# A two-layer trunk with three token mixers on eight cores: the Silu inputs of the branches computed as seven block products

## The chip, the cores and the metric

The program runs on the eight NeuronCores of one Trainium2 chip. Each core computes 1024 of the 8192 tokens, with 62 tokens of left context (a halo), and the cores don't talk to each other. The metric is the device time in microseconds (us) of the slowest core. TensorE (PE) multiplies matrices into PSUM (8 banks of 128 x 512 float32), VectorE (DVE) and ScalarE (ACT) do the elementwise work, the queue of GpSimd (POOL) issues the loads of the weights, SyncE (SP) the other transfers. Each engine runs its own instructions in the order in which the program emits them.

## The reference

```
for each of 2 layers:
  xn = RMSNorm(h)                                # h: tokens x 2048
  proj = xn @ W_in                               # 9 slices of 1024 columns, 3 gates of 2048
  A: y_A = silu(z_A) * B * conv3(C * x_in)
  B: y_B = silu(z_B) * scale * group_linear(trailing_mean_w(u) - u),  w in (2,4,8,16)
  C: y_C = silu(LayerNorm(dwconv31(value * sigmoid(gate)))) * silu(z_C)
  merged = sum over the branches of sigmoid(g_b) * (y_b @ W_branch_out_b)
  h = h + merged @ W_o
  h = h + sigmoid(h @ W_ple_gate) * (p_i @ W_ple_proj)
final RMSNorm
```

The change is about the three inputs z_A, z_B and z_C of silu: products of xn (2048 deep) with 1024 columns of W_in each.

## The kernel before, in words

Channels lie on partitions and tokens along the free axis. xn is 16 tiles of 128 channels x TL = 1086 tokens in bf16. Layer 0 needs 1056 output columns of each tile (LO = 30), layer 1 needs 1024 (LO = 62).

**Plain projection** (`mm_group`, line 308): a tile of 128 output channels is 16 matmuls deep (k = 0..15), over 3 pieces of 352 columns in 3 PSUM banks (layer 0) or 2 of 512 in 2 banks (layer 1). `next_pg` hands out banks in turn. One load (`load_main`, three ring slots) brings the weights of two tiles, which are written "a pair" or "j" here.

**Seven block products** (`block_group`, line 594): a pair is a 2 x 2 block product (two output tiles, two halves of the depth, two halves of the tokens), and one level of Strassen-Winograd makes it from seven products instead of eight: 7 x 8 x 2 matmuls of 264 columns in layer 0 (`nb` = 2), 7 x 8 of 512 in layer 1. It needs sums of the weights, made on VectorE by `weight_sums` (four operations, one of them in place in the ring slot) into the shared `sb`, and sums of xn, made once for each layer by `xsum` into `tb`. On TensorE its products go in the order b0, b4, b1, b0, b2, b1, b2 (banks). In between, ScalarE copies p1 <- p0 ahead of the third product, then saves p4, copies p2 <- p1 ahead of the fifth, applies the function to g00 and saves `u3`. VectorE makes g01 and g11 (two TT) after the sixth product, and ScalarE applies the function to g10; the function on g01 and g11 waits in `pend`. Before the change only the 24 pairs of merge gates of a layer were done in this way (`merge_branch`, line 659), all with Sigmoid.

**Merge of a branch**: for q = 0..3 two gate pairs as block products, then four groups (jj) of 8-deep matmuls of yb, whose PSUM VectorE multiplies by the gate into `acc` (branch A) or into a scratch tile and then adds (B, C). Weight sums of the next gate pair come after the first block, and at jj = 1; those of a branch's first pair stand at the head of `merge_branch`.

**Background taps**: the 31-tap convolution of branch C runs on VectorE. `conv_tap` operations (8 tiles x 31) stand in a queue `bgq`, and `bg(n)` emits the next n at that place of VectorE's order. Eight `xsum` operations are put at the queue's head when branch A begins. `bg(len(bgq))` (line 826) emits all that are left before branch C's LayerNorm, which needs the last tap of the last tile: V(7).

**Branch A** (line 729): for j = 0..3 projections x and C (pieces of 353 or 342), then B, then z: two plain groups, `ACT Silu` from PSUM into Tt, and a product into yb on VectorE. bg(3), bg(1), bg(3), bg(3) follow the tiles of the four projections.

**Branch B** (line 769): u (two tiles, 3 banks each), pooling on VectorE, then z (two plain groups, Silu, bg(3) each), then the small matmuls of `pool_w` into PSUM, read by one STT for each tile into yb. The next j begins with its u groups.

**Branch C** (line 811): z of pair 0, two sums over channels by matmuls with ones, mu and rstd on VectorE and ScalarE (Ln, Exp), then for every tile `cz_norm`: two TT on VectorE, Silu on ScalarE, one TT into yb. For j = 1..3 plain z groups and norms alternate by tile.

Of the kernel before, what the change touches and what calls it, by code (L numbers as in the profile page):

```python
# [15 lines left out]
E = 1024  # L16
# [143 lines left out]
def build_program(depth_run=DEPTH):  # L160
# [41 lines left out]
    with ExitStack() as es:  # L202
# [48 lines left out]
        def TF(i):  # L251
            return Tt[:, i, :], [r_Ta[i], r_Tb[i]]
# [289 lines left out]
        for l in range(depth_run):  # L542
# [48 lines left out]
                TT(q(1, 0), q(0, 0), q(1, 0), ALU.subtract, [rr], [r_S3[slot]])  # L591
                TT(sb[:, 2], q(0, 1), sb[:, 1], ALU.subtract, [rr, r_S[1]], [r_S[2]])

            def block_group(slot, rows, base, pend):
                b0, b4, b1, b2 = (base + i * nb for i in range(4))

                def bank(b):
                    return psa[:, b:b + nb, 0:N], r_bank[b:b + nb]

                def half(row, hf):  # L600
                    ap, res = TF(row)
                    return ap[:, LO + hf * H:LO + hf * H + H].rearrange("p (j n) -> p j n", n=N), [res[hf]]

                def prod(b, lhs, rhs, start):
                    for k in range(8):
                        w, r_w = lhs(k)
                        x, r_x = rhs(k)
                        for j in range(nb):
                            S.op("pe", "matmul", dict(out=psa[:, b + j, 0:N], lhsT=w, rhs=x[:, j * N:(j + 1) * N], start=start and k == 0, stop=k == 7,
                                                      skip_group_check=True), r_w + (r_x if isinstance(r_x, list) else [r_x]), [r_bank[b + j]])  # L610
                    if start:
                        bits[b:b + nb] = [N] * nb

                def wq(i, j, res=None):
# [18 lines left out]
                ua, r_u = TF(4 + rows[0] // 2)  # L633
                u3 = ua[:, 0:H].rearrange("p (j n) -> p j n", n=N)
# [3 lines left out]
                g11, r11 = half(rows[1], 1)  # L638
                prod(b0, wq(0, 0), xh(0, 0), True)
# [8 lines left out]
                ACT(g00, p0, AF.Sigmoid, q0, r00)  # L648
# [3 lines left out]
                TT(g01, p1, g11, ALU.add, q1 + r11, r01)  # L652
                TT(g11, u3, g11, ALU.add, r_u + r11, r11)
                prod(b2, wq(1, 1), xt(3), False)
                ACT(g10, p2, AF.Sigmoid, q2, r10)
                pend.append(lambda: ACT(g01, g01, AF.Sigmoid, r01, r01))
                pend.append(lambda: ACT(g11, g11, AF.Sigmoid, r11, r11))

            def merge_branch(b):
                def load_gate(i):  # L660
                    return load_main(wl[36 + b * 8 + i], 16)

                pend = deque()
                slot = load_gate(0)
                weight_sums(slot)
                for q in range(4):
                    nxt = load_gate(2 * q + 1)
                    block_group(slot, (0, 1), 0, pend)
# [4 lines left out]
                    block_group(slot, (2, 3), 0 if nb == 2 else 4, pend)  # L673
                    bg(4)
                    if q < 3:
                        slot = load_gate(2 * q + 2)
                    elif b == 2:
                        reload(range(10))
                    while pend:
# [2 lines left out]
                    for jj in range(4):  # L682
# [46 lines left out]
            for j in range(4):  # L729
# [12 lines left out]
                for i in range(2):  # L742
# [16 lines left out]
                slot = load_main(wl[(3 * E + u[0] * 128) // 256], 16)  # L759
                for i in range(2):  # L760
                    g = mm_group(proj_steps(slot, i * 128, xn, r_xn), R_out)
                    sz, r_sz = tA[i]
                    co, r_co = cv[i]
                    ACT(v3(sz, R_out), pv(g, R_out), AF.Silu, g.res, r_sz)
                    TT(yb[:, u[i], LO:TL], co[:, LO:TL], sz[:, LO:TL], ALU.mult, r_co + r_sz, [r_yb[u[i]]])
                    bg(3)
            merge_branch(0)

            for j in range(4):
                u = [2 * j, 2 * j + 1]  # L770
# [3 lines left out]
                XY = [TF(2), TF(3)]  # L774
                P = [TB(4, 0), TB(4, 1)]
                slot = load_main(wl[(4 * E + u[0] * 128) // 256], 16)
                for i in range(2):
                    g = mm_group(proj_steps(slot, i * 128, xn, r_xn), RP)
                    Ui, r_Ui = U[i]
# [18 lines left out]
                slot = load_main(wl[(5 * E + u[0] * 128) // 256], 16)  # L798
                for i in range(2):
                    g = mm_group(proj_steps(slot, i * 128, xn, r_xn), R_out)  # L800
                    ACT(v3(U[i][0], R_out), pv(g, R_out), AF.Silu, g.res, U[i][1])
                    bg(3)
                ss = load_side(pool_w[l, j])
                for o in range(2):
                    steps = [(side[:, ss, i, o * 128:(o + 1) * 128], P[i][0], 0, [r_side[ss]] + P[i][1]) for i in range(2)]
                    g = mm_group(steps, R_out)
                    STT(v3(yb[:, u[o], :], R_out), pv(g, R_out), pcol(PB + 24 + u[o]), v3(U[o][0], R_out), ALU.mult, ALU.mult,
                        g.res + [r_par] + U[o][1], [r_yb[u[o]]])
            merge_branch(1)

            def cz_proj(jj, i):
                g = mm_group(proj_steps(cz_slot[jj], i * 128, xn, r_xn), R_out)
                Z, r_Z = TF(i)
                ACT(v3(Z, R_out), pv(g, R_out), AF.Silu, g.res, r_Z)
                return 2 * jj + i, Z, r_Z

            def cz_norm(ui, Z, r_Z):
                a, r_a = TF(2)
# [8 lines left out]
            cz_slot = {0: load_main(wl[(8 * E) // 256], 16)}  # L827
            pre = [cz_proj(0, 0), cz_proj(0, 1)]
# [24 lines left out]
            for o in pre:  # L853
                cz_norm(*o)
            for j in range(1, 4):
                cz_slot[j] = load_main(wl[(8 * E + 2 * j * 128) // 256], 16)
                for i in range(2):
                    cz_norm(*cz_proj(j, i))
            reload(range(10, 16))
            merge_branch(2)  # L860

            for q in (5, 6, 7, 0, 1, 2, 3, 4):
                slot = load_main(w_o[l, q], 16)
# [195 lines left out]
```

How the kernel before makes its waits and increments, by code:

```python
                def body(eng, ops=ops, e=e):  # L105
# [15 lines left out]
                            todo.append((key, val))  # L121
                        emb = None
                        if o.meth is not None and not o.is_dma:
                            for t in todo:
                                if t[0][0] == "e":
                                    emb = t
                            if emb is not None:
                                todo.remove(emb)
                        for key, val in todo:
                            sem = dma_sems[key[1]] if key[0] == "d" else sems[key[1]]
                            eng.wait_ge(sem, val)
                        if o.meth is None:
                            continue
                        ins = getattr(eng, o.meth)(**o.kw)
                        if emb is not None:
                            ins._wait_ge(sems[emb[0][1]], emb[1])
                        if o.is_dma:
                            ins.then_inc(dma_sems[o.dsem], 16)
                        elif o.signal:
                            ins.then_inc(sems[e], 1)
```

## Time and profile before

| | us |
|---|---|
| median of three runs (2591.72 to 2593.22) | 2592.05 |
| the profiled execution, whole | 2592.57 |
| its span on the slowest core (core 1) | 2591.0 |
| spans of the eight cores | 2585.6 to 2591.0 |
| TensorE busy in the span | 2512.6 |
| VectorE busy | 1560.5 |
| ScalarE busy | 556.6 |

The mean granted TensorE clock was 0.992 to 0.993 of full on all cores. All recorded operations show one line (L134, the emitter), so the operations are told apart by their tiles, shapes and times. A timeline row is: start in us from the span's start, length in us, engine, line, operation, output<-input, shape, count, and in brackets the idle time before it and what ended it. The length of a matmul row includes the end of its last matmul, some 0.15 us, which lies beside the next row.

### The profile page before, as it was taken

How to read it: one execution, taken by the hardware profiler on the slowest of the kernel's cores; microseconds unless marked ns; L12 is line 12 of the kernel's file. 1: busy time of each engine (PE TensorE's matmuls, PEld its weight loads, DVE VectorE, ACT ScalarE, POOL GpSimd, SP SyncE). 2: the span in 40 equal slices, each digit the busy share in tenths (PEclk: the TensorE clock that was granted, in tenths of full speed). 3: DMA queues.
4: the chain of work that ended last, by engine and by line, in shares of the span. 5: the costliest groups of instructions: out<-in, count | busy, mean ns of one | idle time of the engine just before them, and what ended most of it. 6: DMA issues, size and time to landing. Idle time of an engine off the chain costs nothing.

```text
span 2591.0 us, 35103 instructions; the slowest of 8 cores (2585.6 to 2591.0 us)
## 1 busy us (share of the span) xinstructions
PE 2512.6 (97%) x15468; PEld 1506.6 (58%) x15468; DVE 1560.5 (60%) x1534; ACT 556.6 (21%) x746; POOL 119.4 (5%) x217
## 2 busy tenths in 40 slices
PE   5999999999999999999999999999999999999997
PEld 2666667776667678766666655544554444444445
DVE  4567666865787753412447676777668885442156
ACT  6000002211212322112340000022112224221124
POOL 0000000000000000000000000000000000000001
PEclk9999999999999999999999999999999999999998
DMA  7434343444344444645553434334434444446453
GB/s 219 88 66 79 69 76 72 82 75 73 73 74 83 92 85 82 143 99 95 132 131 74 75 72 82 73 74 81 86 70 81 91 90 98 83 96 148 84 94 131
DMA packets 49848, 237.51 MB, mean 92 GB/s; under 512 B 4768, under 2 KB 18080, under 8 KB 26912
## 3 DMA queue, kind: packets, MB, share of 16 engines
q0 software_dynamic: 29056, 186.72, 40.1%
q1 hardware_dynamic: 20640, 48.54, 5.6%
q8 instruction: 122, 2.00, 0.3%
q14 instruction: 30, 0.25, 0.0%
HBM read 404.67 MB, written 17.29 MB: 163 GB/s over the span
## 4 chain that ended last, share of the span: by engine, by line
PE 89%; DVE 7%; ACT 1%; SPq 1%; issue 1%; DMA 1%; POOL 0%; DVEq 0%; ACTq 0%; POOLq 0%
PE psa L134 89%; DVE Tt L134 3%; DVE h L134 3%; SPq L134 1%; ACT Tt L134 1%; DVE yb L134 1%; DMA yb<-w_in 1%; DVE acc L134 0%; ACT L134 0%; POOL ring L134 0%; ACT psa L134 0%; ACT yb L134 0%; ACT acc L134 0%; DVEq L131 0%; DVEq L99 0%
## 5 line engine op out<-in xcount | busy, mean ns | idle before, releaser
L134 PE MATMUL psa<-xn,ring 128*128 128x352 bf16 (+8 forms) x8384 | 1365.4, 322 | 9.2 <-DVE Tt L134 5.3
L134 PEld LDWEIGHTS psa<-xn,ring 128*128 128x128 bf16 x8384 | 815.5, 97 | 541.6 <-DVE Tt L134 9.5
L134 DVE SCALAR_TENSOR_TENSOR h<-h,par_s 128x1056 f32<-128x1056 bf16 (+1 forms) x480 | 623.6, 1299 | 11.5
L134 DVE TENSOR_TENSOR Tt<-psa,Tt 128x1056 f32<-128x1056 f32 (+7 forms) x208 | 205.5, 989 | 517.1 <-PE psa L134 477.2
L134 ACT ACTIVATE Tt<-psa 128x512 f32<-128x512 f32 (+9 forms) x328 | 243.2, 742 | 1134.6 <-PE psa L134 1108.2
L134 PE MATMUL psa<-yb,ring 128*128 128x352 bf16 (+1 forms) x1920 | 343.5, 339 | 0.0
L134 PE MATMUL psa<-acc,ring 128*128 128x352 bf16 (+2 forms) x1664 | 292.7, 336 | 31.1 <-DVE acc L134 23.6
L134 PEld LDWEIGHTS psa<-yb,ring 128*128 128x128 bf16 x1920 | 186.5, 97 | 152.2
L134 PEld LDWEIGHTS psa<-acc,ring 128*128 128x128 bf16 x1664 | 161.9, 98 | 159.9 <-DVE acc L134 26.1
L134 DVE TENSOR_TENSOR Tt<-Tt 128x1056 f32<-128x1056 f32 (+9 forms) x130 | 136.0, 1046 | 121.3 <-ACT Tt L134 118.3
L134 PE MATMUL psa<-h 128*128 128x264 bf16 (+1 forms) x1152 | 185.1, 319 | 17.6 <-DVE h L134 16.0
L134 PE MATMUL psa<-h,ring 128*128 128x264 bf16 (+1 forms) x1152 | 184.9, 310 | 0.0
L134 PEld LDWEIGHTS psa<-h 128*128 128x128 bf16 x1152 | 114.4, 100 | 81.4 <-DVE h L134 18.4
L134 DVE TENSOR_TENSOR h<-psa,h 128x1056 f32<-128x1056 f32 (+1 forms) x32 | 39.7, 1241 | 183.9 <-PE psa L134 183.9
L134 PEld LDWEIGHTS psa<-h,ring 128*128 128x128 bf16 x1152 | 112.6, 98 | 56.7
L134 POOL DMA_DIRECT2D ring<-w_in x118 | 62.6, 531 | 1574.9 <-PE psa L134 1251.3
L134 ACT ACTIVATE psa<-psa 128x528 f32<-128x528 f32 (+1 forms) x96 | 56.5, 588 | 361.9 <-PE psa L134 281.2
L134 PE MATMUL psa<-xn,h 128*128 128x264 bf16 (+1 forms) x576 | 92.8, 310 | 0.0
L134 ACT ACTIVATE Tt<-Tt 128x528 f32<-128x528 f32 (+5 forms) x114 | 73.0, 685 | 45.6 <-DVE Tt L134 45.3
L134 ACT ACTIVATE xn<-h 128x1056 bf16<-128x1056 f32 (+1 forms) x32 | 34.2, 1070 | 221.7 <-DVE h L134 221.7
L134 DVE TENSOR_TENSOR acc<-acc,Tt 128x1056 bf16<-128x1056 bf16 (+1 forms) x64 | 79.5, 1242 | 2.2
L134 DVE TENSOR_TENSOR yb<-Tt 128x1056 bf16<-128x1056 f32 (+1 forms) x32 | 39.7, 1242 | 65.0 <-ACT Tt L134 65.0
(70 smaller groups left out, 928.9 us busy)
## 6 DMA issues: line engine op xcount, KB each, us to landing
ring<-w_in POOLq DMA_DIRECT2D x118, 1024.0 KB, 9.0
ring<-w_branch_out POOLq DMA_DIRECT2D x24, 1024.0 KB, 9.0
ring<-w_o POOLq DMA_DIRECT2D x16, 1024.0 KB, 9.6
ring<-w_ple_gate POOLq DMA_DIRECT2D x14, 1024.0 KB, 11.0
h<-xT SPq DMA_DIRECT2D x12, 724.0 KB, 15.7
h<-xT SPq DMA_DIRECT2D x16, 543.0 KB, 8.9
h_keep<-h SPq DMA_DIRECT2D x16, 543.0 KB, 8.8
h<-h_keep SPq DMA_DIRECT2D x16, 543.0 KB, 8.5
```

What stands on the lines that cost most here:

```text
L134: ins = getattr(eng, o.meth)(**o.kw)
```

## The change

- The z pairs of branches A and B in both layers, and those of branch C in layer 1, are computed by `block_group` with Silu: 8 pairs in layer 0, 12 in layer 1. `zbase` is the first PSUM bank: 0 in layer 0 (all eight banks are used), 4 in layer 1.
- The scratch of these blocks (`m5`, `u3`) is the pair's own two tiles of yb seen as float32. In branch B z goes to Tt 5 and to pTs seen as float32.
- Their weight sums stand after the first B tile (A), after the pooling of the first u tile (B), and before the norms of the pair before (C).
- The first gate pair of a merge is loaded ahead of the last z block, and its weight sums follow that block on VectorE (in layer 0's branch C, the last plain z pair).
- Counts of `bg` change: B tiles of branch A from 3 to 2 each, the merge's from 6 + 4 + 4 x 1 to 6 + 5 + 2 for each q, and branch B's from 3 + 3 before the end of z to 6 behind the z block.
- In branch C both z tiles of a pair now come before the two norms, in both layers.

The diff, cut (the two Silu z groups of A and B, and `cz_proj`, are what the new lines replace):

```diff
-            def block_group(slot, rows, base, pend):
+            def block_group(slot, rows, base, pend, func=AF.Sigmoid, m5=None, u3=None):
...
-                ACT(g11, p4, AF.Copy, q4, r11)
+                ACT(m5v, p4, AF.Copy, q4, r_m)
...
-                ACT(g10, p2, AF.Sigmoid, q2, r10)
+                ACT(g10, p2, func, q2, r10)
...
-                slot = load_gate(0)
-                weight_sums(slot)
                 for q in range(4):
...
-                    bg(4)
+                    bg(5)
...
-                        bg(1)
+                        if jj == 0:
+                            bg(2)
...
+            zbase = 0 if nb == 2 else 4
```

Branch A, behind the x and C tiles:

```diff
+                z_slot = load_main(wl[(3 * E + u[0] * 128) // 256], 16)
+                state["pg"] = 0
                 for i in range(2):
                     g = mm_group(proj_steps(slot, i * 128, xn, r_xn), R_out)
...
+                    if i == 0:
+                        weight_sums(z_slot)
+                    bg(2)
+                if j == 3:
+                    slot = load_gate(0, 0)
+                pend = deque()
+                block_group(z_slot, tA, zbase, pend, AF.Silu, yscratch(u[0]), yscratch(u[1]))
+                if j == 3:
+                    weight_sums(slot)
+                while pend:
+                    pend.popleft()()
+                for i in range(2):
+                    TT(yb[:, u[i], LO:TL], cv[i][0][:, LO:TL], tA[i][0][:, LO:TL], ALU.mult, cv[i][1] + tA[i][1], [r_yb[u[i]]])
                     bg(3)
```

Branch B, behind the pooling:

```diff
+                    if i == 0:
+                        weight_sums(z_slot)
+                if j == 3:
+                    slot = load_gate(1, 0)
+                pend = deque()
+                block_group(z_slot, Z, zbase, pend, AF.Silu, yscratch(u[0]), yscratch(u[1]))
+                if j == 3:
+                    weight_sums(slot)
+                while pend:
+                    pend.popleft()()
+                bg(6)
+                state["pg"] = 0
                 ss = load_side(pool_w[l, j])
                 for o in range(2):
```

Branch C:

```diff
+            def cz_block(j, nxt):
...
+                block_group(cz_slot[j], (TF(0), TF(1)), zbase, pend, AF.Silu, yscratch(2 * j), yscratch(2 * j + 1))
+                if nxt is not None:
+                    weight_sums(nxt)
+                while pend:
+                    pend.popleft()()
...
+            cz_slot = [load_main(wl[(8 * E) // 256], 16)]
+            if l > 0:
+                weight_sums(cz_slot[0])
             bg(len(bgq))
+            cz_slot.append(load_main(wl[(8 * E + 256) // 256], 16))
+            cz_block(0, cz_slot[1])
...
             for j in range(1, 4):
+                cz_slot.append(load_main(wl[(8 * E + (j + 1) * 256) // 256], 16) if j < 3 else load_gate(2, 0))
+                cz_block(j, cz_slot[j + 1])
                 for i in range(2):
-                    cz_norm(*cz_proj(j, i))
+                    cz_norm(2 * j + i, *TF(i))
```

## Rows read from the trace of the kernel before

**Rows 1.** The page: busy us of each engine, share of the span, instructions
```profile
PE 2512.6 (97%) x15468; PEld 1506.6 (58%) x15468; DVE 1560.5 (60%) x1534; ACT 556.6 (21%) x746; POOL 119.4 (5%) x217
```

**Rows 2.** Timeline, TensorE, layer 0, merge A: start, us, what [idle before <-releaser]
```profile
495.54 1.97 PE L134 MATMUL psa<-xn,ring 128*128 128x264 bf16 x16
...
508.17 14.59 PE L134 MATMUL psa<-yb,ring 128*128 128x352 bf16 x96
...
522.60 1.98 PE L134 MATMUL psa<-xn,ring 128*128 128x264 bf16 x16
```

**Rows 3.** Timeline, TensorE, layer 1, merge of branch A
```profile
1698.27 1.89 PE L134 MATMUL psa<-xn,ring 128*128 128x512 bf16 x8
...
1710.36 14.03 PE L134 MATMUL psa<-yb,ring 128*128 128x512 bf16 x64
```

**Rows 4.** Timeline, VectorE, the same stretch as rows 2
```profile
508.01 5.38 DVE L134 SCALAR_TENSOR_TENSOR h<-h,par_s 128x1056 f32<-128x1056 bf16 x4
...
513.30 1.25 DVE L134 TENSOR_TENSOR acc<-psa,Tt 128x1056 bf16<-128x1056 f32 x1
...
516.87 0.68 DVE L134 TENSOR_TENSOR h<-ring 128x1024 bf16<-128x1024 bf16 x1
...
519.40 1.31 DVE L134 SCALAR_TENSOR_TENSOR h<-h,par_s 128x1056 f32<-128x1056 bf16 x1
```

**Rows 5.** Timeline, layer 0, branch B, second pair of channel tiles (j=1)
```profile
594.01 29.33 PE L134 MATMUL psa<-xn,ring 128*128 128x357 bf16 x192
...
614.23 8.08 DVE L134 SCALAR_TENSOR_TENSOR h<-h,par_s 128x1056 f32<-128x1056 bf16 x6
...
624.34 2.75 DVE L134 SCALAR_TENSOR_TENSOR yb<-psa,par_s,Tt 128x1056 bf16<-128x1056 f32 x2 [2.03 <-PE psa L134]
...
625.72 29.33 PE L134 MATMUL psa<-xn,ring 128*128 128x357 bf16 x192
```

**Rows 6.** Timeline, layer 1, branch B, j=1
```profile
1883.74 1.04 ACT L134 ACTIVATE Tt<-psa 128x1041 f32<-128x1041 f32 x1 [6.13 <-PE psa L134]
...
1898.43 2.48 DVE L134 SCALAR_TENSOR_TENSOR yb<-psa,par_s,Tt 128x1024 bf16<-128x1024 f32 x2 [1.74 <-PE psa L134]
...
1899.86 28.35 PE L134 MATMUL psa<-xn,ring 128*128 128x347 bf16 x160 [0.67 <-DVE yb L134]
```

**Rows 7.** Timeline, TensorE, layer 0, merge of branch B, one q
```profile
714.65 14.59 PE L134 MATMUL psa<-yb,ring 128*128 128x352 bf16 x96
...
731.00 1.99 PE L134 MATMUL psa<-xn,ring 128*128 128x264 bf16 x16 [1.76 <-DVE Tt L134]
```

**Rows 8.** Timeline, VectorE, layer 0, from branch B to LayerNorm
```profile
860.30 5.37 DVE L134 SCALAR_TENSOR_TENSOR h<-h,par_s 128x1056 f32<-128x1056 bf16 x4
...
874.31 1.26 DVE L134 TENSOR_SCALAR Tt<-psa 128x1056 f32<-128x1056 f32 x1 [8.63 <-PE psa L134]
```

**Rows 9.** Timeline, layer 1, branch C: VectorE, ScalarE, then TensorE
```profile
2117.95 5.24 DVE L134 SCALAR_TENSOR_TENSOR h<-h,par_s 128x1024 f32<-128x1024 bf16 x4
...
2131.14 1.22 DVE L134 TENSOR_SCALAR Tt<-psa 128x1024 f32<-128x1024 f32 x1 [7.95 <-PE psa L134]
...
2149.18 1.24 ACT L134 ACTIVATE Tt<-Tt,par_s 128x1024 f32<-128x1024 f32 x1 [3.75 <-DVE Tt L134]
...
2154.17 1.24 ACT L134 ACTIVATE Tt<-Tt,par_s 128x1024 f32<-128x1024 f32 x1 [2.84 <-DVE Tt L134]
...
2187.29 1.89 PE L134 MATMUL psa<-xn,ring 128*128 128x512 bf16 x8
```

**Rows 10.** Timeline, TensorE, first gate block of branch A's merge, layers 0 and 1
```profile
403.64 5.44 PE L134 MATMUL psa<-h 128*128 128x264 bf16 x32 [5.00 <-DVE h L134]
...
1685.37 6.16 PE L134 MATMUL psa<-h 128*128 128x512 bf16 x16 [5.14 <-DVE h L134]
```

**Rows 11.** Windows, TensorE: stretch, us, busy (count), granted clock, DMA share, GB/s
```profile
406.00:407.00 1.00, 1.00 (x6) 0.50 0.00 0
407.00:408.00 1.00, 1.00 (x10) 0.94 0.00 0
```

More of the change, by code:

```diff
@@ L592, in weight_sums, with yscratch @@
                 TT(sb[:, 2], q(0, 1), sb[:, 1], ALU.subtract, [rr, r_S[1]], [r_S[2]])
-            def block_group(slot, rows, base, pend):
+            def yscratch(k):
+                return yb[:, k, :].bitcast(F32), [r_yb[k]]
+            def block_group(slot, rows, base, pend, func=AF.Sigmoid, m5=None, u3=None):
                 b0, b4, b1, b2 = (base + i * nb for i in range(4))
@@ L598, in bank, with tiled @@
                     return psa[:, b:b + nb, 0:N], r_bank[b:b + nb]
+                def tiled(ap):
+                    return ap.rearrange("p (j n) -> p j n", n=N)
                 def half(row, hf):
-                    ap, res = TF(row)
-                    return ap[:, LO + hf * H:LO + hf * H + H].rearrange("p (j n) -> p j n", n=N), [res[hf]]
+                    ap, res = row
+                    return tiled(ap[:, LO + hf * H:LO + hf * H + H]), [res[hf % len(res)]]
                 def prod(b, lhs, rhs, start):
@@ L632, in block_group @@
                 p4, q4 = bank(b4)
-                ua, r_u = TF(4 + rows[0] // 2)
-                u3 = ua[:, 0:H].rearrange("p (j n) -> p j n", n=N)
+                ua, r_u = u3
+                u3 = tiled(ua[:, 0:H])
                 g00, r00 = half(rows[0], 0)
@@ L638, in block_group @@
                 g11, r11 = half(rows[1], 1)
+                if m5 is None:
+                    m5v, r_m = g11, r11
+                else:
+                    m5v, r_m = tiled(m5[0][:, 0:H]), m5[1]
                 prod(b0, wq(0, 0), xh(0, 0), True)
@@ L647, in block_group @@
                 prod(b0, wq(0, 1), xh(1, 0), False)
-                ACT(g00, p0, AF.Sigmoid, q0, r00)
+                ACT(g00, p0, func, q0, r00)
                 prod(b2, wq(1, 0, r_S3[slot]), xt(2), False)
@@ L651, in block_group, with load_gate, merge_branch @@
                 prod(b1, ws(2), xh(1, 1), False)
-                TT(g01, p1, g11, ALU.add, q1 + r11, r01)
-                TT(g11, u3, g11, ALU.add, r_u + r11, r11)
+                TT(g01, p1, m5v, ALU.add, q1 + r_m, r01)
+                TT(g11, u3, m5v, ALU.add, r_u + r_m, r11)
                 prod(b2, wq(1, 1), xt(3), False)
-                ACT(g10, p2, AF.Sigmoid, q2, r10)
[L656 to L661, printed above, removed]
+                ACT(g10, p2, func, q2, r10)
+                pend.append(lambda: ACT(g01, g01, func, r01, r01))
+                pend.append(lambda: ACT(g11, g11, func, r11, r11))
+            def load_gate(b, i):
+                return load_main(wl[36 + b * 8 + i], 16)
+            def merge_branch(b, slot):
                 pend = deque()
-                slot = load_gate(0)
-                weight_sums(slot)
                 for q in range(4):
-                    nxt = load_gate(2 * q + 1)
-                    block_group(slot, (0, 1), 0, pend)
+                    nxt = load_gate(b, 2 * q + 1)
+                    block_group(slot, (TF(0), TF(1)), 0, pend, u3=TF(4))
                     weight_sums(nxt)
@@ L672, in merge_branch @@
                     bo = load_main512(w_bo[l, b, q])
-                    block_group(slot, (2, 3), 0 if nb == 2 else 4, pend)
-                    bg(4)
+                    block_group(slot, (TF(2), TF(3)), 0 if nb == 2 else 4, pend, u3=TF(5))
+                    bg(5)
                     if q < 3:
-                        slot = load_gate(2 * q + 2)
+                        slot = load_gate(b, 2 * q + 2)
                     elif b == 2:
@@ L757, in build_program @@
                     TT(v3(co, R_out), pv(g, R_out), v3(co, R_out), ALU.mult, g.res + r_co, r_co)
-                    bg(3)
[L759 to L767, printed above, removed]
+                    if i == 0:
[11 more added lines that the diff above has]
+                    TT(yb[:, u[i], LO:TL], cv[i][0][:, LO:TL], tA[i][0][:, LO:TL], ALU.mult, cv[i][1] + tA[i][1], [r_yb[u[i]]])
+                    bg(3)
+                state["pg"] = 0
+            merge_branch(0, slot)
             for j in range(4):
@@ L776, in build_program @@
                 slot = load_main(wl[(4 * E + u[0] * 128) // 256], 16)
+                z_slot = load_main(wl[(5 * E + u[0] * 128) // 256], 16)
+                Z = [TF(5), (pTs[:, :, :].rearrange("p a t -> p (a t)").bitcast(F32), [r_p])]
                 for i in range(2):
@@ L797, in build_program @@
                     TT(Pi[:, HALO:HALO + 16], tmp16[:, :], Ui[:, HALO:HALO + 16], ALU.subtract, [r_tmp16] + r_Ui, r_Pi)
[L798 to L802, printed above, removed]
+                    if i == 0:
[9 more added lines that the diff above has]
+                bg(6)
+                state["pg"] = 0
                 ss = load_side(pool_w[l, j])
@@ L806, in build_program @@
                     g = mm_group(steps, R_out)
[L807 to L815, printed above, removed]
+                    STT(v3(yb[:, u[o], :], R_out), pv(g, R_out), pcol(PB + 24 + u[o]), v3(Z[o][0], R_out), ALU.mult, ALU.mult,
+                        g.res + [r_par] + Z[o][1], [r_yb[u[o]]])
+                state["pg"] = 0
+            merge_branch(1, slot)
+            def cz_block(j, nxt):
+                pend = deque()
+                if l == 0:
+                    for i in range(2):
+                        g = mm_group(proj_steps(cz_slot[j], i * 128, xn, r_xn), R_out)
+                        Z, r_Z = TF(i)
+                        ACT(v3(Z, R_out), pv(g, R_out), AF.Silu, g.res, r_Z)
+                    if j == 3:
+                        weight_sums(nxt)
+                    return
+                block_group(cz_slot[j], (TF(0), TF(1)), zbase, pend, AF.Silu, yscratch(2 * j), yscratch(2 * j + 1))
+                if nxt is not None:
+                    weight_sums(nxt)
+                while pend:
+                    pend.popleft()()
             def cz_norm(ui, Z, r_Z):
@@ L824, in cz_norm @@
                 TT(yb[:, ui, LO:TL], s[:, LO:TL], Z[:, LO:TL], ALU.mult, r_s + r_Z, [r_yb[ui]])
+            cz_slot = [load_main(wl[(8 * E) // 256], 16)]
+            if l > 0:
+                weight_sums(cz_slot[0])
             bg(len(bgq))
[L827 to L828 removed]
+            cz_slot.append(load_main(wl[(8 * E + 256) // 256], 16))
+            cz_block(0, cz_slot[1])
+            if l > 0:
+                state["pg"] = 0
             steps = [(ones[:, :], VH(k)[0], 0, [r_ones] + VH(k)[1]) for k in range(8)]
@@ L852, in build_program @@
             ACT(rstd[:, LO:TL], rstd[:, LO:TL], AF.Exp, r_rstd, r_rstd, scale=-0.5)
-            for o in pre:
-                cz_norm(*o)
+            for i in range(2):
+                cz_norm(i, *TF(i))
             for j in range(1, 4):
-                cz_slot[j] = load_main(wl[(8 * E + 2 * j * 128) // 256], 16)
+                cz_slot.append(load_main(wl[(8 * E + (j + 1) * 256) // 256], 16) if j < 3 else load_gate(2, 0))
+                cz_block(j, cz_slot[j + 1])
                 for i in range(2):
-                    cz_norm(*cz_proj(j, i))
+                    cz_norm(2 * j + i, *TF(i))
             reload(range(10, 16))
-            merge_branch(2)
+            merge_branch(2, cz_slot[4])
             for q in (5, 6, 7, 0, 1, 2, 3, 4):
```

## The prediction

> **What bounds the kernel now.** I read the page first: TensorE is busy for 2512.6 of 2591.0 us and VectorE for 1560.5 [rows 1], so columns of matmuls set the time wherever nothing holds TensorE up, and VectorE looks as if it had room. Then the timeline of each stage, engine by engine, for what stands behind what. The reader should see there that VectorE works in the order of emission: at 508.01 it starts four background taps as soon as it is through with a gate block's two TT, just before that block's last matmul ends, and the eviction behind them starts only at 513.30 [rows 4]. Its spare time therefore helps only where the order lets work run ahead.
>
> **Columns saved.** In layer 0 a gate block takes 508.17 - 495.54 = 12.63 us, and 96 matmuls of 352 columns, what a plain z pair has too, take 522.60 - 508.17 = 14.43 [rows 2]: 1.80 less for each pair. In layer 1 a block takes 1710.36 - 1698.27 = 12.09; the 64 plain matmuls behind it have 14.03 in their row, less the 0.17 that lies beside the next (14.59 against 14.43 in rows 2), so 13.86: 1.77 less [rows 3]. 8 x 1.80 + 12 x 1.77 = 35.6 us saved if nothing else moved.
>
> The Trainium skill speaks against the second of these (TensorE: Matmul & The Clock Gate, Back-to-back issue gap): a sustained stream in real kernels would need about 131 ns for a matmul of 512 columns. Row 3 has 13.86 / 64 = 217 ns, so I stay with it; by that figure eight matmuls fewer would be worth 1.05 us, and the sum would be 9 us higher.
>
> **Branch A.** TensorE first works through the B tiles; weight sums (2.53 us, 516.87 to 519.40 [rows 4]) and two taps lie between two evictions that are 7.2 us apart, and fit. The products into yb and their 3 + 3 taps now come behind the block (they waited for Silu before, too), but the next reader of that Tt is an x tile over 7 us later. So all 1.80 is gained: -4 x 1.80 + 0.2 for matmuls that set flags in fresh banks = -7.0 in layer 0, and -4 x 1.77 + 0.4 = -6.7 in layer 1. The new operations (Silu and Copy of 512 or 528 columns, TT on yb seen as float32) are of the block's known shapes; none is on the path, so I price them as their gate twins and a gain or loss within 0.1 each as nothing.
>
> **Start of A's merge.** Before, the second product waits 5.00 us for weight sums and then 32 matmuls take 5.28 (to 408.92, 5.44 in the row less 0.16) instead of 2 x 1.81: 6.7 in all; in layer 1 it is 5.14 and 6.00 (6.16 less 0.16) instead of 3.45: 7.7 [rows 10]. After, the sums come in time, but ScalarE's save of p4 into Tt 1 waits for the second yb product. On VectorE from the z block's end: 2.4 (sums left) + 1.2 (yb) + 4.0 (three taps) + 1.2 (yb) = 8.8, then 0.6 save and 0.5 copy of p2: the fifth product starts at 9.85 instead of 7.24, 2.6 late, and the clock (below) falls in such a stall for 1.7. -6.7 + 4.3 = -2.4 and, with 2.7 + 1.7, -7.7 + 4.4 = -3.3.
>
> **A's and B's merge in layer 0.** Five taps (4 are 5.29, [rows 4]; 5 are 6.61) stand ahead of the first eviction instead of four. Banks come round in (0, 3, 0, 5): jj = 2 waits for that eviction, 0.5 us late in A. With 2 taps behind jj = 0 the next ones drift too: +0.6 for each q, +2.4. In B each jj has two TT; a q ends 1.76 us late already [rows 7]. Going through the same order, TT 2 ends at 714.49 + 6.61 + 2.46 + 2.55 + 2.46 + 2.53 + 1.28 = 732.38 instead of 730.98, and the third product, which waits for ScalarE and the fourth TT, at +0.7: three q, +2.2; the fourth is in the flush. In layer 1 every group has banks of its own: 0.
>
> **Branch B: the taps behind the block.** This is the first large term. Before, six taps ran during the z groups (614.23 to 622.3) and the STT came at 624.34, on time; the next u group began at 625.72, 31.71 after the last [rows 5]. After, the block's two TT stand ahead of the six taps, and they wait for its sixth product. From the first u matmul: u 14.70, block to 27.33, TT done 27.17, six taps to 35.1, STT of tile 0 to 36.45, and the next u group, in the same banks 0 to 2, at 36.5. That is +4.8 with the column gain inside, for j = 0, 1, 2: +14.4. For j = 3 there are 2.53 of sums as well, so merge B starts at 39.05 instead of 31.9: +7.1. Layer 0: +21.5.
> Layer 1: u is 3 banks (0 to 2, 3 to 5) and z's first product goes to bank 4, which ScalarE clears only with its copy of u, 1.04 long, 0.3 after the last u matmul [rows 6]: TensorE stands 1.37. Block to 14.33 + 1.37 + 12.09 = 27.8; TT to 27.6, six taps (7.75) to 35.4, both STT (2.4; bank 2 belongs to the second) to 37.8; next u at 37.85. Before it was 30.76 (two STT in 2.48, u 1.4 behind their start [rows 6]). 3 x 7.1 = +21.3; for j = 3, with sums, and one STT, b0 of the merge comes +8.2 late. Layer 1: +29.5.
>
> **Flush.** 8 x 31 + 8 = 256 entries. Before, 37 go in the value stage, 4 x 20 in A, 56 in a merge, 24 in B, 56: 3 are left; the row at 860.30 shows them with the merge's last one, x4 [rows 8]. After: 256 - 37 - 72 - 52 - 24 - 52 = 19 left. In layer 0 the merge's end comes at 860.7, 19 x 1.3225 = 25.1 bring V(7) to 885.9, and mu follows 0.7 later at 886.6 instead of 874.31: +12.3, where taps before ended at 865.7, long before need. With slow matmuls behind it +12.8.
> Layer 0's branch C end: Silu of both z tiles now stands ahead of the first norm. For j = 3 it waits for the last z matmul, so two norms (5.1 each) come behind, and ScalarE's copy of p1 behind these: the third product 4.3 late, plus clock, against 2.4 and clock before: +2.0.
>
> **Branch C in layer 1.** The second large term. From 2099.75: weight sums, 19 taps (24.5), block 0's two TT (1.3), again weight sums (2.4), then mu at 2148.9 instead of 2131.14 [rows 9]: 17.7 late. From there each block hangs on the norms: ScalarE's copy of p1, ahead of the third product, stands behind the second Silu of the norms of the pair before. That Silu ends at 2150.4 + 17.7 = 2168.1 [rows 9], so block 1's third product starts at 2168.7. Then four products 6.9, two TT 1.5, sums 2.4, two norms from first TT to last Silu 3.8 + 4.99 = 8.8 (the pace of 2149.18 to 2154.17 [rows 9]), copy 0.6: 20.3 for each. Three of these: 2229.7, and the merge's fourth product at 2231.5 instead of 2187.29 [rows 9]: +44.2, with flags +44.6.
>
> **The clock.** Behind a 5 us wait the granted clock is 0.50, the 1.2 GHz level, until about 407.1, and then back at 2.4 GHz [rows 11]; 32 matmuls lose 5.28 - 3.61 = 1.7, in layer 1 6.00 - 3.45 = 2.55 [rows 10]. New stalls of 7 to 11 us: 8 in branch B, 4 in C. I take the 1.7 of layer 0: 12 x 1.7 = +20.4; between 0 and 2.55 each it is 0 to +31.
>
> The Trainium skill's rule (same page, HAM oscillation) has each idle gap leave some 1.67 us at half clock, half of it lost: 0.8 for each, 10 us in all. The rows show twice that; by the rule the sum is 10 lower.
>
> **Sum.** Layer 0: -7.0 - 2.4 + 2.4 + 21.5 + 2.2 + 12.8 + 2.0 = +31.5. Layer 1: -6.7 - 3.3 + 29.5 + 44.6 = +64.1. Clock +20.4. Together +116.0 on the profiled execution's own 2592.57 (span 2591.0 and 1.6 around it), 2708.6; that execution is 0.5 above the median of 2592.05, so 2708.
>
> **Rivals.**
> (1) The chains as above, but TensorE loses nothing to its clock: 2688. For it: waits of 1.76 [rows 7] leave no trace. Against: both rows of 5 us do.
> (2) Branch C's blocks don't hang on the norms, because TensorE or ScalarE gets ahead of them: then of +44.6 only the late mu (17.7) less three pairs (5.3) and the merge's wait (4.4) stay, and 4 x 1.7 go: 2708 - 36.6 - 6.8 = 2665. Against: ScalarE has one order, and the copy is behind Silu there.
> (3) Columns decide. VectorE is 60% busy; if its idle time takes up taps and sums, all 35.6 is gained, and up to 14.4 more at the starts of A's merge: 2542 to 2556. It decides once the delays add up to less than 35.6. Against it: the six taps of branch B (8 us) can't run ahead of TT that wait for the block, and eight times 8 us is more than that alone.
> (4) Something on top: spells of low clock of 5 us everywhere (+11) with a weight load that comes late: beyond 2730.
>
> **How the numbers follow.** Forecast 66% (its own range 2694 to 2722), (1) 10%, (2) 8%, (3) 5%, (4) 9%, savings and delays equal 2%. The range 2674 to 2730 takes in the forecast, (1), and errors of 10% in the two large chains. A measurement tells 0.2%, 5 us, from no change: faster 5%, same 2%, slower 93%.
>
> **What would show it.** In branch B six taps stand between the block's second TT and the STT, and TensorE stands 7 us or more ahead of each u group, at clock 0.5 after. In layer 0 nineteen taps run in a row and mu begins some 12 us after TensorE is through with z. In layer 1's branch C the third products are 20 us apart. Gate blocks and z blocks take 12.63 and 12.09. If the STT follows the TT at once, or the taps before the flush are few, I am wrong; if third products are 12 apart, it is (2).

## The result and the profile after

The changed kernel takes 2718.84 us (median of four executions, 2718.27 to 2719.81) against 2592.51 for the kernel before, a ratio of 1.0488 [1.0470, 1.0506]: 126.3 us slower, where 116.0 was forecast. The profiled execution has a span of 2718.2 us, 127.2 more than before. (Some executions run with the cores of one die at a lower clock; the ratios leave the clear cases out, so a median over all of a kernel's executions can stand apart from its ratio.) The kernel before took 2592.5 beside this one, 2594.5 beside e1 to e4, 2593.0 beside a_only, ab_ordered, abc_ordered and ab_tuned, and 2594.4 beside abc_split and abc_piped, so a difference between kernels of different groups is good to some 2 us.

The page, busy line, and TensorE's waits (engine, tile, what ended the wait: us in total, times, longest):

```profile
PE 2511.4 (92%) x15504; PEld 1518.8 (56%) x15504; DVE 1638.8 (60%) x1654; ACT 607.7 (22%) x866; POOL 119.4 (4%) x217
...
PE psa L134 <- DVE yb L134: 63.8, 8, 9.6
PE psa L134 <- ACT psa L134: 44.2, 7, 11.3
PE psa L134 <- DVE h L134: 26.4, 3, 13.3
```

TensorE's busy time is what it was [rows 1]: the 35 us of matmuls that went are made up by other matmuls at half clock (27.5 us of it behind the twelve long stalls, see The clock below). The waits are new. Those before were, for the same three:

```profile
PE psa L134 <- DVE h L134: 16.0, 5, 5.1
...
PE psa L134 <- DVE yb L134: 2.0, 3, 0.7
PE psa L134 <- ACT psa L134: 1.6, 3, 0.5
```

Branch B, layer 0, j = 1 (the stretch of rows 5): TensorE, then VectorE.

```profile
591.71 18.38 PE L134 MATMUL psa<-xn,ring 128*128 128x357 bf16 x112 [6.49 <-DVE yb L134]
609.93 3.76 PE L134 MATMUL psa<-h 128*128 128x264 bf16 x32
...
620.75 1.98 PE L134 MATMUL psa<-Tt,side 128*128 128x352 bf16 x12
629.83 10.47 PE L134 MATMUL psa<-xn,ring 128*128 128x357 bf16 x58 [7.10 <-DVE yb L134]
```
```profile
619.22 0.71 DVE L134 TENSOR_TENSOR Tt<-psa,yb 128x528 f32<-128x528 f32 x1 [5.64 <-PE psa L134]
619.85 0.70 DVE L134 TENSOR_TENSOR pTs<-yb 128x528 f32<-128x528 f32 x1
620.46 8.08 DVE L134 SCALAR_TENSOR_TENSOR h<-h,par_s 128x1056 f32<-128x1056 bf16 x6
628.46 1.31 DVE L134 SCALAR_TENSOR_TENSOR yb<-psa,par_s,Tt 128x1056 bf16<-128x1056 f32 x1
```

The reader should see VectorE idle for 5.64 us, with six taps ready that need nothing of the block, and the taps starting only when the block's own two TT are done. The pooling matmuls are through at 622.7; what empties their banks comes behind 8.08 us of taps, and TensorE stands for 7.10. From u group to u group it is 629.83 - 591.71 = 38.12 instead of 31.71.

Layer 0, VectorE and TensorE ahead of LayerNorm (rows 8):

```profile
885.27 25.68 DVE L134 SCALAR_TENSOR_TENSOR h<-h,par_s 128x1056 f32<-128x1056 bf16 x19
912.12 1.26 DVE L134 TENSOR_SCALAR Tt<-psa 128x1056 f32<-128x1056 f32 x1 [1.16 <-PE psa L134]
```
```profile
896.97 3.33 PE L134 MATMUL psa<-h,ones_s 128*128 128x352 bf16 x21
911.02 1.06 PE L134 MATMUL psa<-h,ones_s 128*128 128x352 bf16 x3 [10.72 <-DVE h L134]
911.87 1.09 PE L134 MATMUL psa<-Tt,ones_s 128*128 128x352 bf16 x3
914.05 5.95 PE L134 MATMUL psa<-Tt,ones_s 128*128 128x352 bf16 x21 [1.09 <-DVE Tt L134]
```

Twenty-one matmuls take 3.33 ahead of the wait and 5.95 behind it: the same shape, at a granted clock of 0.50 until 918 and of 0.64 from there to 920.

Layer 1, branch C (rows 9): ScalarE around the third product of the second block, then TensorE's third products.

```profile
2240.98 1.24 ACT L134 ACTIVATE Tt<-Tt,par_s 128x1024 f32<-128x1024 f32 x1 [3.75 <-DVE Tt L134]
2242.12 0.58 ACT L134 ACTIVATE psa<-psa 128x512 f32<-128x512 f32 x1
```
```profile
2229.61 1.89 PE L134 MATMUL psa<-h 128*128 128x512 bf16 x8
2242.76 3.59 PE L134 MATMUL psa<-h 128*128 128x512 bf16 x8 [11.26 <-ACT psa L134]
...
2265.22 3.60 PE L134 MATMUL psa<-h 128*128 128x512 bf16 x8 [8.01 <-ACT psa L134]
...
2288.39 3.48 PE L134 MATMUL psa<-h 128*128 128x512 bf16 x8 [8.01 <-ACT psa L134]
...
2310.24 3.59 PE L134 MATMUL psa<-h 128*128 128x512 bf16 x8 [7.58 <-ACT psa L134]
```

The copy of p1 (2242.12) starts the moment the second Silu of a norm ends, and the third product starts when the copy does. TensorE had been ready since 2231.5.

By stage, from the same marks on TensorE in both traces, core 1 in each (the forecast with its clock terms):

| stretch | measured | forecast |
|---|---|---|
| L0 A and start of its merge | -9.0 | -9.4 |
| L0 merge A | +2.6 | +2.4 |
| L0 branch B and the merge's first products | +29.1 | +28.3 |
| L0 merge B | +3.8 | +4.2 |
| L0 LayerNorm (wait for the taps) | +14.0 | +10.8 |
| L0 rest of C | +2.7 | +2.0 |
| L1 A and start of its merge | -10.1 | -10.0 |
| L1 merges A and B | 0.0 | 0.0 |
| L1 branch B | +38.6 | +36.3 |
| L1 branch C | +54.6 | +51.4 |

These add up to 126.3; 0.9 more lies in the next product of C's merge (2.83 instead of 1.89, at half clock). The first row counts from the span's start, and the first projection began 0.7 later than before (75.86 against 75.14), so the stage itself gave -9.8. Of merge B's +4.2 and LayerNorm's +10.8, 2.0 is a split of the flush's 12.8 between them.

### The profile page after: what moved, and what is told of

It reads as the page before. It is cut to its first block, busy times and chain, and to the rows that moved or that the text cites. A ratio compares the mean times of both kernels' runs of the same rounds, so it can differ in the third digit from the quotient of the medians.

```text
span 2718.2 us, 35460 instructions; the slowest of 8 cores (2712.8 to 2718.2 us)
## 1 busy us (share of the span) xinstructions
PE 2511.4 (92%) x15504; PEld 1518.8 (56%) x15504; DVE 1638.8 (60%) x1654; ACT 607.7 (22%) x866; POOL 119.4 (4%) x217
## 4 chain that ended last, share of the span: by engine, by line
PE 83%; DVE 12%; issue 1%; ACT 1%; SPq 1%; DMA 1%; POOL 0%; DVEq 0%; ACTq 0%; POOLq 0%
PE psa L134 83%; DVE h L134 7%; DVE Tt L134 3%; SPq L134 1%; DVE yb L134 1%; ACT Tt L134 1%; DMA yb<-w_in 1%; DVE acc L134 0%; DVE ring L134 0%; DVE pTs L134 0%; ACT psa L134 0%; ACT L134 0%; POOL ring L134 0%; ACT yb L134 0%; ACT acc L134 0%
## 5 line engine op out<-in xcount | busy, mean ns | idle before, releaser
L134 PE MATMUL psa<-xn,ring 128*128 128x352 bf16 (+8 forms) x7296 | 1180.3, 321 | 74.4 <-DVE yb L134 63.8
L134 PEld LDWEIGHTS psa<-xn,ring 128*128 128x128 bf16 x7296 | 716.4, 98 | 517.2 <-DVE yb L134 67.2
L134 ACT ACTIVATE Tt<-psa 128x528 f32<-128x528 f32 (+8 forms) x320 | 221.2, 692 | 892.9 <-PE psa L134 864.5
L134 PE MATMUL psa<-h 128*128 128x264 bf16 (+1 forms) x1600 | 261.4, 321 | 41.6 <-ACT psa L134 39.2
L134 PE MATMUL psa<-h,ring 128*128 128x264 bf16 (+1 forms) x1600 | 264.1, 315 | 5.0 <-ACT psa L134 5.0
L134 PEld LDWEIGHTS psa<-h 128*128 128x128 bf16 x1600 | 158.8, 100 | 132.0 <-ACT psa L134 41.5
L134 ACT ACTIVATE psa<-psa 128x512 f32<-128x512 f32 (+1 forms) x136 | 80.1, 589 | 669.9 <-PE psa L134 598.5
L134 PEld LDWEIGHTS psa<-h,ring 128*128 128x128 bf16 x1600 | 157.0, 98 | 89.6 <-ACT psa L134 5.8
L134 ACT ACTIVATE Tt<-Tt 128x512 f32<-128x512 f32 (+5 forms) x146 | 92.0, 673 | 64.1 <-DVE Tt L134 63.9
L134 PEld LDWEIGHTS psa<-xn,h 128*128 128x128 bf16 x800 | 78.4, 98 | 43.3 <-issue 1.3
```

Source lines behind the costliest of these rows:

```text
L134: ins = getattr(eng, o.meth)(**o.kw)
```

## The experiments

The first three kernels undo one thing each, and the fourth takes the clock's part away. The theory was the forecast's: three orders on two in-order queues, and the clock behind each stall.

**e1_taps_behind_stt**: branch B's six taps behind the pooling's STT.

```diff
-                bg(6)
                 state["pg"] = 0
...
                         g.res + [r_par] + Z[o][1], [r_yb[u[o]]])
                 state["pg"] = 0
+                bg(6)
```

> The changed kernel with one line moved: branch B's six taps stand behind the two STT of the pool matmuls instead of ahead of them; nothing else differs. Theory (VectorE's order: the STT that free the banks of the next u group wait for taps that wait for the block): the stall ahead of each u group falls from 6.5 to 9.6 us to about 1 in layer 0 and 2 in layer 1 (the STT then wait only for Silu of g01 and g11), with it the low clock behind it; 75 us less than the changed kernel, 2644. Rival (the u group waits for Silu, the block or the pool matmuls anyway, the taps only fill that time): within 15 us of 2719.

2651.35 us, 1.0220 [1.0202, 1.0238]: 67.5 less than the changed kernel. The wait behind VectorE's yb falls from 63.8 us to 12.5; those behind ScalarE's psa (44.2) and VectorE's h (26.4, now 24.7) stay.

```profile
PE psa L134 <- DVE yb L134: 12.5, 8, 2.1
```
```profile
614.70 1.98 PE L134 MATMUL psa<-Tt,side 128*128 128x352 bf16 x12
617.59 16.71 PE L134 MATMUL psa<-xn,ring 128*128 128x357 bf16 x112 [0.92 <-DVE yb L134]
```

The wait is 0.92 and the u matmuls that take 18.38 above take 16.71: no spell of half clock. The order of six instructions is worth half the loss. The 75 expected was too much: the waits give 51.3, the half clock behind the eight stalls 18.2 (see The clock), and 1.7 comes back behind one of the waits that are left (last section), which makes 67.8.

**e2_counts_of_before**: the counts of `bg` as before, so three taps are left at the flush.

```diff
-                    bg(5)
+                    bg(4)
...
-                        if jj == 0:
-                            bg(2)
+                        bg(1)
...
-                    bg(2)
+                    bg(3)
```

> The changed kernel with the numbers of background taps as before the change in branch A (3 behind each B tile) and in the merges (6 + 4 + 4 x 1 for each q); in branch B the six stay where the change has them. 3 instead of 19 taps are then left for the flush. Theory: mu comes about 12 us earlier in layer 0 and 17 in layer 1, layer 0's merges lose their waits for banks (2.6 and 3.8 us), and clock behind the flush is full: about 40 us less than 2719, 2679. Rival (mu waits for something else, the z block or its weight sums, and the flush lies beside it): under 15 us less.

2683.15, 1.0341 [1.0320, 1.0361]: 35.7 less. By stage the traces have 14.0 ahead of layer 0's LayerNorm and 16.7 in layer 1's branch C (from the last yb row of merge B to the first of merge C, 162.10 and 145.42), both the flush, and 6.4 in layer 0's merges, whose evictions no longer stand behind an added tap. The wait on VectorE's h falls to one of 4.4 us; in layer 0 the sums over channels run through:

```profile
890.96 3.77 PE L134 MATMUL psa<-h,ones_s 128*128 128x352 bf16 x24
...
896.70 3.33 PE L134 MATMUL psa<-Tt,ones_s 128*128 128x352 bf16 x21 [1.51 <-DVE Tt L134]
```

**e3_c_plain**: z of branch C plain in layer 1 too.

```diff
-                if l == 0:
+                if True:
...
-            if l > 0:
-                weight_sums(cz_slot[0])
```

> The changed kernel with branch C's z as plain groups in layer 1 too (both tiles of a pair ahead of their norms, as layer 0 has it); A, B and all tap counts as changed. It does 4 x 8 x 512 more columns. Theory (each block of branch C waits for the norms of the pair before, over ScalarE's copy): third products 22 us apart are replaced by plain groups of 13.9, branch C of layer 1 keeps only the flush and is 36 to 40 us shorter: 2681. Rival (the flush and LayerNorm cost it, and blocks save columns): 7 us slower than 2719.

2682.27, 1.0340 [1.0322, 1.0358]: 36.6 less; TensorE's wait on ScalarE's psa falls from 44.2 us to 13.7. Its flush is untouched, so this is the loss of C's blocks beside a late mu; by the traces 37.3 of it lie in that branch.

**e4_filler**: no order is changed; matmuls with no use are laid into the waits of B and C, so that TensorE stays busy until its banks come.

```diff
+                fill(7, ((46, 52, 52, 74), (30, 32, 32, 38))[l][j])
             merge_branch(1, slot)
...
+                fill((base + 4) % 8, nfill)
                 prod(b1, ws(1), xt(1), False)
```

> The changed kernel with matmuls that nobody reads (ones times xn, into a bank that is free then) in most of each long stall of TensorE: 30 to 74 of them behind the pool matmuls in branch B, 30 to 46 ahead of the third product in branch C's blocks of layer 1 and in the first block of its merge. No wait is shortened by it. Theory (behind each stall TensorE runs at the lower clock level and loses 1.4 to 2.9 us on the path): the granted clock stays at 1.00 behind the stalls, and 12 stalls x 2.3 = 27 us go: 2692. Rival (the work behind a stall is slow for another reason, or its loss is not on the path): 2719 or more.

2691.46, 1.0375 [1.0355, 1.0395]: 27.4 less by work *added* to TensorE. Filler, then the u group at full speed at the same place:

```profile
621.49 6.02 PE L134 MATMUL psa<-xn,ones_s 128*128 128x264 bf16 x52
628.76 16.70 PE L134 MATMUL psa<-xn,ring 128*128 128x357 bf16 x112 [1.25 <-DVE yb L134]
```

Twelve waits were filled, so the clock cost 27.4 / 12 = 2.3 us each. Rival (1), a free clock, is refuted by 27 us. With the clock at full behind the stalls, what is left are the chains alone, and they have the forecast's lengths: u groups start 36.46 and 36.44 apart in layer 0 (forecast 36.5), 37.81 twice in layer 1 (37.85), and the third products of branch C 20.3 apart (20.3):

```profile
2223.50 1.90 PE L134 MATMUL psa<-h 128*128 128x512 bf16 x8 [1.33 <-ACT psa L134]
...
2243.77 1.90 PE L134 MATMUL psa<-h 128*128 128x512 bf16 x7 [1.09 <-ACT psa L134]
```

**a_only** and **ab_ordered**: what the blocks give where the order does not hurt. The first has them in branch A alone; the second in A and B, with e1's order, the counts of before, and C as before.

> The kernel before with block products for z in branch A alone, with A's first gate pair loaded and summed ahead; all tap counts as before, branches B and C as before. Theory (only columns and the start of A's merge change; 9.0 us in layer 0 and 10.1 in layer 1 by the changed kernel's timelines): 19 us faster than before. Rival (blocks put enough on VectorE that taps run late and take the columns' gain back): within 5 us of before.

> a_only with branch B's block products as well, its six taps behind the STT; tap counts as before, branch C as before. Theory (by the timelines of the run with the taps moved: layer 0's branch B 5 us shorter than before, layer 1's 4 longer, for a copy of u ahead of the block's bank and a wait for both STT): within 3 us of a_only, 19 to 21 faster than before. Rival (branch B's blocks bring their columns, 14 us): 33 faster.

a_only: 2571.73, 0.9944 [0.9906, 0.9982], six of its ten executions within 2570.4 to 2571.9, some 21.7 under the kernel before; its four terms of the forecast are -19.4. ab_ordered: 2570.02, 0.9910 [0.9893, 0.9927]. Both as expected: A gives what was forecast and 2 more (behind its wait of 2.4 at layer 0's merge the clock fell on none of cores 2 to 7 of the profiled execution, where 1.7 had been put down; see the last section), and B's 8 x 1.8 = 14 us of columns bring under 2: TensorE now waits 12.5 us for the STT there, in eight waits of 0.9 to 2.1.

**abc_ordered**: the changed kernel with e1 and e2 together, C's blocks kept.

> The changed kernel with both cures together: six taps behind the STT, tap counts as before, branch C's blocks of layer 1 kept. Theory (the chain over ScalarE's copy and the norms, with low clock behind each wait, is all that is left of the loss): 36 us slower than ab_ordered, 15 to 20 slower than before; third products still 21 to 23 us apart. Rival (the chain of branch C was set off by the flush and goes with it): at ab_ordered's time or 5 under it.

Executions of 2615.2 to 2615.6, 1.0087 [1.0062, 1.0111]: 103.3 under the changed kernel, and e1 and e2 alone give 67.5 + 35.7 = 103.2. By the ratios it is 104 against 108, so the two orders are independent to within some 4 us. Against ab_ordered it is 46 slower, where 36 was expected. By the traces 39.2 of these lie in layer 1's branch C (145.69 against 106.50 from the last yb row of merge B to the first of merge C): the third term, where 7.1 of columns should have been saved. Another 2.9 lie in layer 0's branch C, whose new order (both z tiles ahead of the norms) this kernel keeps and ab_ordered doesn't; the rest lies in the start of the span and in stages that the edit leaves alone.

**abc_split**: the same, with the norms of the pair before emitted behind the block's third product, so that the copy of p1 is ahead of their Silus. It leaves out a buffer that it would need: the second half of z's last tile is overwritten by the merge's first block before it is used, so that part of the result is not the program's. Its instructions and their number are the same, so the time can be compared.

```diff
+                    cz_block(j, cz_slot[j + 1], {"b1": lambda j=j: norms(j - 1)})
...
+            merge_branch(2, cz_slot[4], {} if l == 0 else {"b1": lambda: (norms(3), reload(range(10, 16)))})
```

> Both orders cured and branch C still as block products in layer 1 (abc_ordered, 19 to 24 us slower than the kernel before), with one change: the LayerNorm of the pair of block columns before is emitted behind the block's third product, so the copy psa p1<-p0 and the saving of p4 no longer stand in ScalarE's queue behind its Silus. Theory (what holds up the third product is that copy's place in the queue): the wait of 7.6 to 11.3 us ahead of every third product goes, a part comes back two products later ahead of the fifth (2 products are 3.5 us), and each of the four blocks gets some 3.5 us shorter: 14 us less than abc_ordered, ratio to before about 1.003. Rival (VectorE's chain of the norms alone sets the period of a block, whatever the queue): the wait only changes its place, and the time is that of abc_ordered within 3 us, ratio about 1.008.

2601.49, 1.0028 [1.0018, 1.0038]: some 14 under abc_ordered, as the theory had it. The wait is now on the fifth product, and shorter:

```profile
2159.22 2.74 PE L134 MATMUL psa<-h,ring 128*128 128x512 bf16 x6 [4.48 <-ACT psa L134]
...
2177.98 3.19 PE L134 MATMUL psa<-h,ring 128*128 128x512 bf16 x7 [4.88 <-ACT psa L134]
```

A block takes 18.4 to 18.9 us instead of 21.8 to 23.2. So ScalarE's order does set the period, but emitting the norms later only chooses which product waits for them.

**ab_tuned**: ab_ordered with other orders and banks, against the waits that remain.

```diff
-                    bg(3)
+                    bg((0, 6)[i] if j == 3 else 3)
...
+                    if nb == 1:
+                        state["pg"] = 5 * i
...
-                block_group(z_slot, Z, zbase, pend, AF.Silu, yscratch(u[0]), yscratch(u[1]))
+                block_group(z_slot, Z, 0, pend, AF.Silu, yscratch(u[0]), yscratch(u[1]))
...
-                state["pg"] = 0
+                state["pg"] = 0 if nb == 2 else 4
...
-                bg(6)
+                bg((6, 6, 4, 8)[j])
```

In branch C the weight sums for the merge also stand ahead of the last norm's product.

> ab_ordered with what the timelines still show as waits taken away by order and banks: A's last two products ahead of six taps; in layer 1 the u groups in banks 0 to 2 and 5 to 7, the block in 0 to 3, the pool matmuls in 4 to 7; taps behind the STT 6, 6, 4, 8; the gate sums of C's merge ahead of its last product. Theory (stalls of 4.3 + 4.3 at A's merge, 0.9 x 3 in layer 0's and 3.4 x 4 in layer 1's branch B, 4 + 4 at C's merge go): 28 to 31 us faster than ab_ordered, 48 to 50 faster than before. Rival (another wait takes their place): under half of it.

**2543.26, 0.9808 [0.9789, 0.9828]: 50 us faster than the kernel before, and the best here.** Against ab_ordered it is 26 to 27, where 28 to 31 was expected: the waits of layer 0's branch B (three of 0.9 and one of 1.64) have stayed. In layer 1 a u group follows the pooling with no wait:

```profile
1884.99 1.90 PE L134 MATMUL psa<-Tt,side 128*128 128x512 bf16 x8
1886.72 14.49 PE L134 MATMUL psa<-xn,ring 128*128 128x347 bf16 x96
```

**abc_piped**: ab_tuned with C's blocks in layer 1, the norms laid in pieces between the products of the next block.

```diff
+                def hk(x):
+                    return {"p1": lambda: (n_s(x), n_y(x), n_tt(x + 1)), "g00": lambda: (n_s(x + 1), n_y(x + 1))}
```

> The kernel ab_tuned (49 us faster than before; branches A and B as block products, C plain) with branch C of layer 1 as block products as well, the norms of one block laid between the products of the next one instead of all in one piece, so that every copy and every addition to a PSUM bank finds its engine free. C plain costs four rows of eight products, the block form seven eighths of it, 14 us of TensorE less (four blocks of 12.1 us against 16 groups of about 3.5 us and their weight loads). Theory (branch C's loss was the order of the side work, not its amount): 8 to 10 us faster than ab_tuned, ratio about 0.977. Rival (VectorE has 11 to 12 us of norms, sums and reads for each block of 12.1 us, so it runs late whatever the order): PSUM banks come late, the clock falls, and the time is that of ab_tuned within 3 us or above it.

The expectation has an error of its own: four rows of eight products against seven eighths of them is 55.4 - 48.5 = 7 us, not 14. It took 2556.28 and 2556.57 in two executions, some 13 more than ab_tuned, and they are too few for a ratio; the spans of the profiled executions agree (2554.7 against 2541.6). The rival had the time right, and more than right:

```profile
2109.99 3.35 PE L134 MATMUL psa<-h,ring 128*128 128x512 bf16 x8 [2.48 <-ACT yb L134]
...
2116.36 3.63 PE L134 MATMUL psa<-h 128*128 128x512 bf16 x16 [1.05 <-DVE h L134]
...
2122.99 1.90 PE L134 MATMUL psa<-h,ring 128*128 128x512 bf16 x8 [1.27 <-ACT psa L134]
```

No wait is over 2.5 us here but one of 4.38 at the flush (block 0's second product, which waits for VectorE's sums). ab_tuned has plain matmuls in both places: 64 in one row beside the flush, and 200 beside the norms.

```profile
2068.29 14.02 PE L134 MATMUL psa<-xn,ring 128*128 128x512 bf16 x64
...
2090.76 43.46 PE L134 MATMUL psa<-xn,ring 128*128 128x512 bf16 x200
```

From z's first matmul to the merge's first yb matmul C takes 99.75 us (2070.26 to 2170.01) against 88.57 (2068.29 to 2156.86): seven saved, eighteen lost. The rival's reason, too much work on VectorE, isn't shown: VectorE is busy for 69 of the 100 us from 2070 to 2170, and the rows above wait for ScalarE and for sums. What a different interleaving would give was not tried.

## Why the prediction was right, and where it was short

**The bound.** Right. The loss lies where VectorE or ScalarE, both under 61% busy, had the needed instruction behind another one.

**Columns.** Right: z and gate blocks last 12.63 and 12.09 as before, and a_only gives the whole of branch A's saving. The Trainium skill's 131 ns for a matmul of 512 columns (TensorE: Matmul & The Clock Gate, Back-to-back issue gap) is what no row read here shows; the 200 above take 43.3 / 200 = 217 ns, at a granted clock of 1.00.

**Branch B.** Right in its chain, to 0.1 us where the clock is out of it (e4): 4.8 forecast for each j in layer 0 without the clock, 38.12 - 31.71 - 1.7 = 4.7 measured; in layer 1 1948.48 to 1988.81 is 40.3 against 30.76, so 9.6 where 7.1 and 1.7 were forecast.

```profile
1948.48 17.03 PE L134 MATMUL psa<-xn,ring 128*128 128x347 bf16 x96 [8.18 <-DVE yb L134]
1966.63 1.90 PE L134 MATMUL psa<-xn,ring 128*128 128x512 bf16 x8 [1.13 <-ACT Tt L134]
...
1988.81 3.66 PE L134 MATMUL psa<-xn,ring 128*128 128x347 bf16 x12 [8.18 <-DVE yb L134]
```

The wait for bank 4 (1.13, forecast 1.37) and the 8.2 us for the STT are as told; the row of 17.03 is 14.49 in ab_tuned, so the half clock took 2.5, and 9.6 - 2.5 is the 7.1 of the chain.

**Flush.** Right in its cause: nineteen taps, mu 12.3 late by forecast and 912.12 - 874.31 = 37.8 less the 26.5 that TensorE was late already, so 11.3, in the trace; e2 gives 14.0 and 16.7 for the two layers. The term was too small in layer 0, by 3.2: only 0.5 was put down for slow matmuls behind the wait, and the 21 of the second sum alone lose 2.6.

**Branch C.** Right in its chain (the copy of p1 behind the second Silu). Third products come 22.5, 23.2 and 21.9 us apart, forecast 20.3 and 1.7 of clock; 20.3 is what e4 has.

**The clock: the mis-sized term.** The forecast took 1.7 for each of twelve stalls, the layer 0 row, though the row of layer 1 said 2.55. The u rows behind the stalls lose 18.38 - 16.70 = 1.7, 1.4 and 2.9 in layer 0, 1.9 to 2.8 in layer 1, the first products of the merges 2.5 and 2.4, and branch C's third products and those behind them 1.6 to 2.9. The twelve add up to 27.5 on core 1, and e4 gives 27.4: 7 us more than the 20.4 forecast. With the 3.2 of the flush these are the 10 that are missing. Granted clock behind two of them (stretch, us, busy, clock, DMA share, GB/s):

```profile
591.70:593.70 2.00, 1.99 (x7) 0.50 0.32 66
593.70:595.70 2.00, 2.00 (x10) 0.63 0.00 0
595.70:597.70 2.00, 2.00 (x16) 1.00 0.00 0
1988.80:1990.80 2.00, 1.99 (x7) 0.50 0.11 17
...
1992.80:1994.80 2.00, 2.00 (x9) 0.54 0.00 0
```

The spell at 1.2 GHz lasts 3.5 us in the first and 5.8 in the second, half of it lost. By the Trainium skill's rule (same page, HAM oscillation), some 1.67 us at half clock for each gap, it would be 0.8 each and 10 us in all (an estimate from the page's figure); e4's 27.4 are against it.

**Rivals.** (2), that C's blocks get clear of the norms, is refuted by the third products and by abc_piped: even with an order made for it they don't. (3), columns decide, is false for this kernel, but it is where ab_tuned arrives: 2543 lies in its 2542 to 2556. In part that is chance, for ab_tuned lacks C's 7 us of columns and gains at the start of C's merge, which (3) didn't count. (4) had one half of what came, longer spells of low clock (7 us of its 11), and not the other: TensorE's one wait for a ring load is as it was (6.2, before 6.4).

## What to carry to other kernels

A busy share of 60% says nothing of whether work can be added; ask for each instruction that empties a PSUM bank what is emitted ahead of it, and whether that waits for something late. Background work belongs behind such an instruction, never between it and the wait that precedes it: here the same six taps, eight times over, cost 67 us in front and nothing visible behind. A saving of matmuls pays only where the extra copies and sums find idle slots of both elementwise engines (branch A: all of it; C beside its LayerNorm: minus 11 us even when interleaved), and here each stall of 6.5 to 11 us came with 1.4 to 2.9 us of half clock on top.

## What was not expected of the hardware

Waits far shorter than the stalls above can also drop the clock, and not each time. The changed kernel has a wait of 2.4 us at the start of A's merge in layer 0, the same on all eight cores of the profiled execution. Core 0 and core 2:

```profile
398.61 3.13 PE L134 MATMUL psa<-h,ring 128*128 128x264 bf16 x16 [2.41 <-ACT psa L134]
```
```profile
397.03 1.97 PE L134 MATMUL psa<-h,ring 128*128 128x264 bf16 x16 [2.42 <-ACT psa L134]
```

From the first projection to the merge's first yb matmul cores 0, 1, 3 and 4 take 343.9 us and the other four 342.2: the fall costs 1.7, on half the cores. The forecast had put down 1.7 there for certain.

e1 has the same 2.12 us wait three times in layer 1's branch B. On core 2 the second is followed by a fall. Its windows of 1 us, TensorE, behind the second and the third:

```profile
1899.80:1900.80 1.00, 1.00 (x7) 1.00 1.24 164
1900.80:1901.80 1.00, 1.00 (x6) 0.50 0.79 147
1901.80:1902.80 1.00, 1.00 (x5) 0.50 1.03 188
...
1933.20:1934.20 1.00, 1.00 (x7) 1.00 1.15 221
```

Behind the second, the matmuls start at 2.4 GHz and fall to 1.2 only a microsecond later, with TensorE busy again; the row takes 16.17 instead of 14.51. Behind the first and the third nothing happens. Each of the eight cores has exactly one such row of 16.2 in the three: five behind the second wait, three behind the third. What decides is open.
